# Two transformer blocks on one core: the up projections of MLP and FFN computed transposed, with the weights stationary

## The chip, the cores and the metric

One Trainium2 chip, one of its cores. The time is that of one execution on the device in microseconds; a lower one is better.

## The reference, cut to what matters

The program runs two transformer blocks in float32 on 256 tokens of width 2048. The first mixes by Fourier transform and attention and has an MLP with squared relu; the second (gated linear attention and a convolution, with modulation from a vector c) ends with a SwiGLU FFN. The parts that the change touches are these:

```python
    u = _rmsnorm(h, norm_mlp_g[layer])               # first block; D = 2048
    a = jnp.einsum('bsd,df->bsf', u, w_up[layer])    # 2048 -> 8192
    a = jnp.square(jax.nn.relu(a))
    h = h + jnp.einsum('bsf,fd->bsd', a, w_down[layer])
...
def swiglu(h, wg, wu, wd):                           # second block
    return (jax.nn.silu(h @ wg) * (h @ wu)) @ wd     # 2048 -> 5632 -> 2048
```

_rmsnorm scales every token by rsqrt(mean(x*x) + eps) and every channel by g.

## The kernel before, in words

**Precision.** A float32 matrix product is made of three fast ones. Each operand is split into a part rounded to float32r (whi, xhi, ahi, bhi) and a remainder (wlo, xlo, alo, blo); the products hi x hi, hi x lo and lo x hi are summed in PSUM.

**Weights.** SyncE streams all weights from HBM into a ring of four slots (wring), each a "group" of 4 depth tiles of 128 by 512 columns (512 KB), in two pieces of two tiles. For each piece ScalarE rounds to whi (round_groups, L488), VectorE subtracts to wlo (remainders, L919), TensorE multiplies. whi and wlo have room for 4 pieces, so the two engines work two groups ahead of TensorE. An engine's program is a fixed order written out by hand; counts kept by the class Counts turn it into semaphore waits.

**A block** is 512 output columns for all 256 tokens: four groups when the depth is 2048. multiply (L1514) holds 128 tokens of the activations stationary and streams 512 columns of weights: for each depth tile and each half t of the tokens three matmuls (L1530, L1531, L1532). So the sums lie in PSUM (acc, two banks for a pair) with tokens on the partitions and columns on the free axis. Two pairs of banks alternate.

**The MLP** (mlp_chunk, on PE L1693, ACT L692, DVE L1152) has 4 chunks of 2048 hidden columns. A chunk is four up blocks (j = 0 to 3, from ahi/alo) and four down blocks (j = 4 to 7, from xhi/xlo, 2048 deep). ScalarE's relu_square (L671) takes max(x, 0) * rstd out of PSUM, one operation for each half of the tokens (L676), and squares into blk (L680). For the down product the hidden columns must be on the partitions. So TensorE turns blk by 8 transposes of 128x128 (turn_rows, L1537, L1545) into the two banks of tp, beside the next block after its second group; ScalarE rounds from there into xhi (round_banks, L503) and VectorE takes the remainder (remain_banks, L959), which frees tp (tp_free). A down block is added to h by VectorE (add_block, L1122, L1124). Beside this VectorE multiplies the modulation matrix w_mod with two vectors, row by row, into macc (L935, L939); POOL loads it, and TensorE sums over partitions with ones (reduce_mod, L1555). The last chunk also turns the context rows for the second block.

**The FFN** (ffn, on PE L1935, ACT L862, DVE L1450) has 11 blocks of hidden columns in chunks of 4, 4 and 3. A hidden block is a gate block (pair 0) and an up block (pair 1). ScalarE takes silu of the gate out of PSUM into blk2 (silu_gate, L856), VectorE multiplies by the up sums out of PSUM into blk (gate_up, L1432, L1435), TensorE turns blk, and ScalarE and VectorE split it into bhi and blo. Four down blocks follow each chunk. The turn of a chunk's last block stands after the second group of the first down block, where its rounding and remainder are needed for the last group. The input of the FFN comes already normed and modulated in xhi/xlo; its first gate block is woven with the turning of the input (ffn_opening, L1916).

**Elsewhere**, which the change leaves alone: block l (multiply_rank, L1499, lines L1508 to L1510) is a projection to 32 columns that holds the 32 columns of weights stationary and streams 256 tokens, in float32r. The Fourier stage (L1608, L1619) has plain float32 matmuls with 128-column weights and about 128 streamed columns.

The loop over the hidden tiles in multiply, for comparison with the new one:

```python
for t in range(T):
    dst = acc[:, 2 * pair + t, :]
    rows = slice(t * P, (t + 1) * P)
    pe.matmul(dst, hi[:, tile, rows], whi[:, h4, w], start=(kg == first and k == 0), stop=False)
    pe.matmul(dst, hi[:, tile, rows], wlo[:, h4, w], start=False, stop=False)
```

## Time and profile before

| | us |
|---|---|
| median of 3 runs | 2341.2 (2340.49 to 2341.93) |
| the profiled execution | 2339.57 |
| its span | 2337.9 |
| TensorE busy | 2294.8 (98%) |
| TensorE's weight loads busy | 1891.3 (81%) |
| VectorE busy | 1541.3 (66%) |
| ScalarE busy | 1079.8 (46%) |

How to read it: PE is TensorE's matmuls, PEld its weight loads, which overlap the matmuls; DVE is VectorE, ACT ScalarE, POOL GpSimd. L1530 is line 1530 of the kernel. A row of a group has its count after x, then the busy time in us and the mean of one in ns, and then the engine's idle time before it. Matmuls are pipelined and the ends of their records are modelled, so the distance between starts, not the length of a record, tells how long one takes. The name on the left of <- is what is written.

### The profile page before, as it was taken

The numbers are of one execution on the slowest core, as the hardware profiler recorded it, in microseconds if no ns is written. First come the engines' busy times: TensorE is split into PE (matmuls) and PEld (weight loads), VectorE is DVE, ScalarE is ACT, GpSimd is POOL, SyncE is SP. The second block draws the span as 40 slices with busy tenths as digits, with TensorE's granted clock in tenths as the row PEclk, the third lists the DMA queues.
The fourth block names the chain that finished last, engine by engine and source line by source line (L and its number), as shares of the span: only waits on it lengthen the run. The fifth ranks groups of instructions, "written<-read, shape, count | busy, mean of one in ns | idle before, by whom it ended". The sixth has DMA issues, their size and how long they took to land.

```text
span 2337.9 us, 29147 instructions
## 1 busy us (share of the span) xinstructions
PE 2294.8 (98%) x10577; PEld 1891.3 (81%) x10577; DVE 1541.3 (66%) x1822; ACT 1079.8 (46%) x1291; POOL 146.2 (6%) x213
## 2 busy tenths in 40 slices
PE   8999999999999999999999999998999999999997
PEld 7887888888888888888878877787888888888886
DVE  7987658777876876886767664566455544455545
ACT  5445445445444444445563463444444344444444
POOL 1110001111111111110011000000000000000000
PEclk9999999999999999999999999999999999999999
DMA  9884458888888888886677663464555655555553
GB/s 340 291 273 155 127 180 300 294 306 272 271 295 267 264 289 272 268 279 215 214 250 242 210 210 126 145 242 154 195 184 191 209 194 188 190 195 188 193 180 108
DMA packets 245186, 523.91 MB, mean 224 GB/s; under 512 B 20016, under 2 KB 20288, under 8 KB 243776
## 3 DMA queue, kind: packets, MB, share of 16 engines
q1 hardware_dynamic: 213680, 404.80, 53.0%
q0 software_dynamic: 29568, 111.97, 13.9%
q10 hardware_dynamic: 1808, 5.37, 0.6%
q8 instruction: 86, 1.41, 0.3%
q14 instruction: 44, 0.36, 0.0%
HBM read 517.87 MB, written 4.21 MB: 223 GB/s over the span
## 4 chain that ended last, share of the span: by engine, by line
PE 97%; ACT 1%; DVE 1%; issue 1%; DMA 0%; ACTq 0%; DVEq 0%
PE acc L1530 30%; PE acc L1532 30%; PE acc L1531 30%; PE tp L1545 2%; PE m L1555 1%; PE acc L1665 0%; PE tp L1839 0%; PE tp L1857 0%; PE tp L1851 0%; PE acc L1629 0%; PE tp L1765 0%; PE m L1639 0%; PE tp L1825 0%; DVE wlo L919 0%; ACT whi L488 0%
## 5 line engine op out<-in xcount | busy, mean ns | idle before, releaser
L919 DVE TENSOR_TENSOR wlo<-wring,whi 128x1024 fp32r<-128x1024 f32 x776 | 935.1, 1214 | 603.9 <-ACT whi L488 600.6
L488 ACT ACTIVATE whi<-wring 128x1024 fp32r<-128x1024 f32 x776 | 813.5, 1052 | 1116.3 <-PE acc L1532 1113.0
L1530 PE MATMUL acc<-whi,xhi 128*128 128x512 f32 x2112 | 832.7, 394 | 2.7 <-issue 1.9
L1532 PE MATMUL acc<-whi,xlo 128*128 128x512 f32 x2112 | 823.4, 390 | 0.0
L1531 PE MATMUL acc<-wlo,xhi 128*128 128x512 f32 x2112 | 822.7, 390 | 0.0
L1530 PEld LDWEIGHTS acc<-whi,xhi 128*128 128x128 f32 x2112 | 397.2, 188 | 93.9 <-issue 12.7
L1532 PEld LDWEIGHTS acc<-whi,xlo 128*128 128x128 f32 x2112 | 396.8, 188 | 83.7
L1531 PEld LDWEIGHTS acc<-wlo,xhi 128*128 128x128 f32 x2112 | 397.4, 188 | 81.0 <-issue 0.7
L939 DVE SCALAR_TENSOR_TENSOR macc<-mring,csil,macc 128x512 f32<-128x512 f32 x480 | 344.2, 747 | 31.8 <-DMA mring<-w_mod 25.4
L1530 PE MATMUL acc<-whi,ahi 128*128 128x512 f32 x608 | 239.0, 393 | 2.0 <-DVE wlo L919 1.2
L1532 PE MATMUL acc<-whi,alo 128*128 128x512 f32 x608 | 237.0, 390 | 0.0
L1531 PE MATMUL acc<-wlo,ahi 128*128 128x512 f32 x608 | 236.6, 389 | 0.0
L427 POOL DMA_DIRECT2D mring<-w_mod x192 | 136.4, 711 | 1118.7 <-DVE macc L939 1097.2
L1530 PE MATMUL acc<-whi,bhi 128*128 128x512 f32 x352 | 137.2, 390 | 1.6 <-DVE blo L959 1.6
L1532 PE MATMUL acc<-whi,blo 128*128 128x512 f32 x352 | 137.0, 389 | 0.0
L1531 PE MATMUL acc<-wlo,bhi 128*128 128x512 f32 x352 | 136.9, 389 | 0.0
L1530 PEld LDWEIGHTS acc<-whi,ahi 128*128 128x128 f32 x608 | 114.2, 188 | 25.5 <-issue 2.7
L1532 PEld LDWEIGHTS acc<-whi,alo 128*128 128x128 f32 x608 | 114.1, 188 | 24.2
L1531 PEld LDWEIGHTS acc<-wlo,ahi 128*128 128x128 f32 x608 | 114.2, 188 | 23.0
L1530 PEld LDWEIGHTS acc<-whi,bhi 128*128 128x128 f32 x352 | 66.1, 188 | 15.4 <-DVE blo L959 1.8
L1532 PEld LDWEIGHTS acc<-whi,blo 128*128 128x128 f32 x352 | 66.1, 188 | 13.8
L1531 PEld LDWEIGHTS acc<-wlo,bhi 128*128 128x128 f32 x352 | 66.1, 188 | 13.6
(221 smaller groups left out, 1027.2 us busy)
## 6 DMA issues: line engine op xcount, KB each, us to landing
wring<-w_up SPq DMA_DIRECT2D x216, 512.0 KB, 4.6
wring<-w_down SPq DMA_DIRECT2D x216, 512.0 KB, 5.1
mring<-w_mod POOLq DMA_DIRECT2D x192, 512.0 KB, 5.2
wring<-w_in SPq DMA_DIRECT2D x184, 512.0 KB, 5.4
wring<-w_gate SPq DMA_DIRECT2D x88, 512.0 KB, 4.2
wring<-w_out SPq DMA_DIRECT2D x64, 512.0 KB, 4.8
gbig<-ctx_in POOLq DMA_DIRECT2D x2, 1024.0 KB, 8.3
hspill<-h ACTq DMA_DIRECT2D x1, 2048.0 KB, 7.9
```

The lines of the kernel that those rows point to most:

```text
L427: pool.dma_start(mring[:, c.slot("m", MSLOTS), :, :], w_mod_v[s, :, :, bass.ds(i * NB + kind * D, NB)])\
L488: act.activation(whi[:, piece_slot(c, piece), 0:half], wring[:, g4, piece * half:(piece + 1) * half], ACT.Copy).then_inc(hi_done, 1)
L919: dve.tensor_tensor(wlo[:, h4, 0:half], wring[:, g4, piece * half:(piece + 1) * half], whi[:, h4, 0:half].bitcast(F32), ALU.subtract).then ...
L939: dve.scalar_tensor_tensor(macc[:, who, :], mring[:, m2, kt, :], csil[:, who, k:k + 1], macc[:, who, :], ALU.mult, ALU.add).then_inc(mod_a ...
L1530: pe.matmul(dst, hi[:, tile, rows], whi[:, h4, w], start=(kg == first and k == 0), stop=False)
L1531: pe.matmul(dst, hi[:, tile, rows], wlo[:, h4, w], start=False, stop=False)
L1532: last = pe.matmul(dst, lo[:, tile, rows], whi[:, h4, w], start=False, stop=(kg == final and k == KG - 1))
L1545: last = pe.transpose(tp[:, q, j * S + t * P:j * S + (t + 1) * P], src[:, t, f:f + P], ident)
L1555: last = pe.matmul(m1[:, 4 * who + j:4 * who + j + 1], macc[:, who, j * P:(j + 1) * P], ones[:, 0:1], start=True, stop=True)
```

## The change

The up projections (MLP) and the gate and up projections (FFN) are computed with the weights stationary. multiply_turned holds 128 columns of weights and streams all 256 tokens, so that the sums come out with hidden columns on the partitions and tokens on the free axis: for a depth tile 4 slices of columns times three matmuls of 256 instead of 2 halves of the tokens times three of 512. Two slices share a bank. blk then has the form that the down product needs; it is not turned. ScalarE rounds it by one operation from blk (round_up), VectorE takes the remainder by one (remainder_up), and the semaphores up_hi and up_lo stand for them. Since tokens lie on the free axis, relu can't take rstd as a scale of the partitions any more; relu_square leaves it out, and the adds of the down blocks multiply by rsq = rstd * rstd (add_scaled). The down blocks stay as they were. The core of the diff:

```diff
@@ -668,17 +672,20 @@
             round_added(3)
             square_added(3 * NB, 3)
 
-            def relu_square(j, first=False):
-
-                if first:
-                    act.wait_ge(rstd_done, 2)
-                for t in range(T):
-                    last = act.activation(blk2[:, t, :], acc[:, 2 * (j % 2) + t, :], ACT.Relu, scale=rstd[:, 1, t:t + 1])
-                last.then_inc(blk_half, 1)
+            def relu_square(j):
+
+                act.wait_ge(up_lo, c.at("up"))
+                act.activation(blk2[:, :, :], acc[:, 2 * (j % 2):2 * (j % 2) + 2, :], ACT.Relu).then_inc(blk_half, 1)
                 c.add("half")
                 act.wait_ge(blk_half, c.at("half"))
                 act.activation(blk[:, :, :], blk2[:, :, :], ACT.Square).then_inc(blk_ready, 1)
                 c.add("blk")
+
+            def round_up(dst, tile):
+
+                act.wait_ge(blk_ready, c.at("blk"))
+                act.activation(dst[:, tile:tile + 4, :], blk_tiles, ACT.Copy).then_inc(up_hi, 1)
+                c.add("up")
 
             def square_block(n, first):
 
...
@@ -1125,6 +1132,20 @@
                                   ALU.add).then_inc(h_added, 1)
 
 
+            def add_scaled(n, pair):
+
+                for t in range(T):
+                    cols = h[:, t, n:n + NB]
+                    last = dve.scalar_tensor_tensor(cols, acc[:, 2 * pair + t, :], rsq[:, t:t + 1], cols, ALU.mult, ALU.add)
+                last.then_inc(h_added, 1)
+
+            def remainder_up(hi, lo, tile):
+
+                c.add("up")
+                dve.wait_ge(up_hi, c.at("up"))
+                dve.tensor_tensor(lo[:, tile:tile + 4, :], blk_tiles, hi[:, tile:tile + 4, :].bitcast(F32),
+                                  ALU.subtract).then_inc(up_lo, 1)
+
             def remain_added(n):
 
                 remain_banks(ahi, alo, 4 * n, 2, lambda k: vecs[:, 0, V_MLPG + k:V_MLPG + k + 1])
...
@@ -1159,8 +1180,10 @@
                         norm_mean(1)
                     elif first and g == 2:
                         norm_root(1, mean=False)
+                        dve.tensor_tensor(rsq[:, :], rstd[:, 1, :], rstd[:, 1, :], ALU.mult).then_inc(rsq_set, 1)
+                        dve.wait_ge(rsq_set, 1)
                     if g % 4 == 1 and 1 <= j <= 4:
-                        remain_banks(xhi, xlo, 4 * (j - 1), 2)
+                        remainder_up(xhi, xlo, 4 * (j - 1))
                     if g in MLP_REDUCED:
                         set_mod(MLP_REDUCED[g], i, MLP_REDUCED[g] == SC1)
                         if last and MLP_REDUCED[g] == SC1:
...
@@ -1432,6 +1455,7 @@
             def gate_up():
 
                 dve.wait_ge(blk_half, c.at("half", 1))
+                dve.wait_ge(up_lo, c.at("up"))
                 dve.tensor_tensor(blk[:, :, :], blk2[:, :, :], acc[:, 2:4, :], ALU.mult).then_inc(blk_ready, 1)
                 c.add("half")
 
...
@@ -1531,6 +1555,26 @@
                                 pe.matmul(dst, hi[:, tile, rows], wlo[:, h4, w], start=False, stop=False)
                                 last = pe.matmul(dst, lo[:, tile, rows], whi[:, h4, w], start=False,
                                                  stop=(kg == final and k == KG - 1))
+                        last.then_inc(piece_multiplied, 1)
+                    c.add("g")
+
+            def multiply_turned(hi, lo, kgs, pair, operand=None):
+
+                for kg in kgs:
+                    for piece in range(SPLIT):
+                        h4 = piece_slot(c, piece)
+                        if operand:
+                            pe.wait_ge(operand[0], operand[1] + piece)
+                        pe.wait_ge(lo_done, c.at("g", SPLIT * WSLOTS + piece + 1, SPLIT))
+                        for j in range(HALF):
+                            tile = kg * KG + piece * HALF + j
+                            for f in range(NB // P):
+                                dst = acc[:, 2 * pair + f // 2, f % 2 * S:(f % 2 + 1) * S]
+                                w = slice(j * NB + f * P, j * NB + (f + 1) * P)
+                                pe.matmul(dst, whi[:, h4, w], hi[:, tile, :], start=(tile == 0 and f % 2 == 0), stop=False)
+                                pe.matmul(dst, whi[:, h4, w], lo[:, tile, :], start=False, stop=False)
+                                last = pe.matmul(dst, wlo[:, h4, w], hi[:, tile, :], start=False,
+                                                 stop=(tile == KT - 1 and f % 2 == 1))
                         last.then_inc(piece_multiplied, 1)
                     c.add("g")
 
...
@@ -1707,20 +1751,26 @@
                         pe.wait_ge(blk_half, c.at("half", j - 1))
                     else:
                         pe.wait_ge(h_added, c.at("ha", 2 + j - 5))
-                    hi, lo = (ahi, alo) if j < 4 else (xhi, xlo)
+                    def group(kg):
+
+                        if j < 4:
+                            multiply_turned(ahi, alo, (kg,), pair)
+                        else:
+                            if j == 4:
+                                c.add("up")
+                                pe.wait_ge(up_lo, c.at("up"))
+                            multiply(xhi, xlo, (kg,), 4, pair)
+
                     for kg in range(3):
-                        multiply(hi, lo, (kg,), 4, pair)
+                        group(kg)
                         if first and j == 0 and kg == 0:
                             turn_added(3)
-                        if kg == 1 and 1 <= j <= 4:
-                            pe.wait_ge(blk_ready, c.at("blk", j))
-                            turn_rows(blk, 2)
                         if 4 * j + kg in MLP_REDUCED:
                             reduce_kind(MLP_REDUCED[4 * j + kg])
                         turn_ctx(4 * j + kg)
-                    if j == 4 or (first and j == 0):
+                    if first and j == 0:
                         pe.wait_ge(tp_free, c.at("q", 2))
-                    multiply(hi, lo, (3,), 4, pair)
+                    group(3)
                     if 4 * j + 3 in MLP_REDUCED:
                         reduce_kind(MLP_REDUCED[4 * j + 3])
                     turn_ctx(4 * j + 3)
...
@@ -1941,26 +1991,19 @@
                     if first and j == 0:
                         ffn_opening()
                     else:
-                        multiply(xhi, xlo, range(2), 4, 0)
-                        if j:
-                            pe.wait_ge(blk_ready, c.at("blk", j))
-                            turn_rows(blk, 2)
-                        multiply(xhi, xlo, (2, 3), 4, 0)
+                        multiply_turned(xhi, xlo, range(4), 0)
                     if not j:
                         pe.wait_ge(h_scaled, c.at("hs"))
-                    multiply(xhi, xlo, range(4), 4, 1)
+                    multiply_turned(xhi, xlo, range(4), 1)
                 for n in range(4):
                     if n == 0:
                         pe.wait_ge(blk_half, c.at("half", blocks))
                     elif n >= 2:
                         pe.wait_ge(h_scaled, c.at("hs", n - 1))
-                    multiply(bhi, blo, range(2), blocks, n % 2)
-                    if n == 0:
-                        pe.wait_ge(blk_ready, c.at("blk", blocks))
-                        turn_rows(blk, 2)
-                    for kg in range(2, blocks):
-                        if n == 0 and kg == blocks - 1:
-                            pe.wait_ge(tp_free, c.at("q", 2))
+                    for kg in range(blocks):
+                        if n == 0:
+                            c.add("up")
+                            pe.wait_ge(up_lo, c.at("up"))
                         multiply(bhi, blo, (kg,), blocks, n % 2)
                 c.add("half", blocks)
                 c.add("blk", blocks)
```

Not shown: the tile rsq and the semaphores are declared; round_banks and remain_banks of blk become round_up and remainder_up at the same places of ScalarE's and VectorE's orders (in mlp_chunk and ffn); add_block of the MLP's down blocks becomes add_scaled; the four calls of multiply in TensorE's ffn_opening become multiply_turned; counts of the loops follow.

## Rows read from the trace of the kernel before

**Rows 1.** the page's busy times (part 1) and granted clock (part 2)
```profile
PE 2294.8 (98%) x10577; PEld 1891.3 (81%) x10577; DVE 1541.3 (66%) x1822; ACT 1079.8 (46%) x1291; POOL 146.2 (6%) x213
...
PEclk9999999999999999999999999999999999999999
```
**Rows 2.** the page's chain that ended last, by line
```profile
PE acc L1530 30%; PE acc L1532 30%; PE acc L1531 30%; PE tp L1545 2%; PE m L1555 1%; PE acc L1665 0%; PE tp L1839 0%; PE tp L1857 0%; PE tp L1851 0%; PE acc L1629 0%; PE tp L1765 0%; PE m L1639 0%; PE tp L1825 0%; DVE wlo L919 0%; ACT whi L488 0%
```
**Rows 3.** list of TensorE's waits: us in total, times, longest
```profile
PE acc L1530 <- DVE blo L959: 1.6, 1, 1.6
```
**Rows 4.** busy times in two stretches: us, then each engine's busy us
```profile
core 0: us, PE busy (x) PEld busy (x) DVE busy (x) ACT busy (x) POOL busy (x), PEclk, DMA share, GB/s
340.00:523.00 183.00, 183.00 (x848) 152.47 (x847) 141.81 (x168) 88.38 (x106) 24.38 (x35) 1.00 0.86 294
1606.00:1860.00 254.00, 254.00 (x1139) 210.67 (x1138) 133.00 (x117) 108.35 (x108) 0.00 (x0) 1.00 0.58 192
```
**Rows 5.** timeline of TensorE in an up block: start us, us, instruction
```profile
899.62 0.39 PE L1530 MATMUL acc<-whi,ahi 128*128 128x512 f32 x1
...
905.97 0.39 PE L1531 MATMUL acc<-wlo,ahi 128*128 128x512 f32 x1
```
**Rows 6.** TensorE groups by line and form: busy us, mean ns, idle before
```profile
L1530 PEld LDWEIGHTS acc<-whi,xhi 128*128 128x128 f32 x2112 | 397.2, 188 | 93.9 <-issue 12.7 <-DVE xlo L979 0.7 <-DVE wlo L919 0.4
...
L1508 PEld LDWEIGHTS acc<-xhi,whi 128*32 128x32 f32 x16 | 1.7, 108 | 0.1
...
L1545 PE MATMUL tp<-tabs,blk 128*128 128x128 f32 x248 | 32.2, 273 | 0.1
```
**Rows 7.** timeline of TensorE around one turn of blk
```profile
373.68 1.04 PE L1545 MATMUL tp<-tabs,blk 128*128 128x128 f32 x8
...
374.47 0.47 PE L1530 MATMUL acc<-whi,ahi 128*128 128x512 f32 x1
...
377.09 0.39 PE L1532 MATMUL acc<-whi,alo 128*128 128x512 f32 x1
```
**Rows 8.** timeline, last FFN chunk: VectorE, then TensorE
```profile
2259.66 1.22 DVE L1435 TENSOR_TENSOR blk<-blk,acc 128x1024 f32<-128x1024 f32 x1
...
2268.05 1.03 PE L1545 MATMUL tp<-tabs,blk 128*128 128x128 f32 x8
...
2270.66 0.50 PE L1530 MATMUL acc<-whi,bhi 128*128 128x512 f32 x1 [1.57 <-DVE blo L959]
```
**Rows 9.** timeline of TensorE in block l: first, fourth and last of 48
```profile
1097.33 0.28 PE L1508 MATMUL acc<-ahi,whi 128*32 128x256 f32 x1
...
1097.68 0.28 PE L1508 MATMUL acc<-ahi,whi 128*32 128x256 f32 x1
...
1102.67 0.28 PE L1510 MATMUL acc<-alo,whi 128*32 128x256 f32 x1
```
**Rows 10.** timeline in the Fourier stage: matmuls, then their weight loads
```profile
197.12 1.95 PE L1608 MATMUL acc<-tab_f,proj 128*128 128x129 f32 x16
...
197.01 1.86 PEld L1608 LDWEIGHTS acc<-tab_f,proj 128*128 128x128 f32 x16
```
**Rows 11.** VectorE groups by line and form: busy us, mean ns, idle before
```profile
L939 DVE SCALAR_TENSOR_TENSOR macc<-mring,csil,macc 128x512 f32<-128x512 f32 x480 | 344.2, 747 | 31.8 <-DMA mring<-w_mod 25.4 <-DVE states L1277 0.7 <-DVE convT L1218 0.4
...
L959 DVE TENSOR_TENSOR xlo<-tp,xhi 128x512 fp32r<-128x512 f32 x32 | 20.5, 682 | 0.0
...
L1239 DVE SCALAR_TENSOR_TENSOR gbig<-tp,gbig 128x512 f32<-128x512 f32 x8 | 5.5, 692 | 19.5 <-ACT gbig L768 19.5
...
L1331 DVE TENSOR_TENSOR xlo<-convT,xhi 128x1024 fp32r<-128x1024 f32 x2 | 2.4, 1222 | 2.1 <-ACT xhi L819 2.1
```
**Rows 12.** timeline of TensorE, one reduction of macc by ones
```profile
933.87 0.95 PE L1555 MATMUL m<-ones,macc 128*128 128x1 f32 x8
```
**Rows 13.** the page's DMA queues (part 3) and issues (part 6)
```profile
q8 instruction: 86, 1.41, 0.3%
...
wring<-w_in SPq DMA_DIRECT2D x8, 64.0 KB, 2.4
```

40 lines of the change are left out of this document (22 added, 18 removed).

## Prediction, made before the change was run

> **What bounds the kernel now.** I read the page's head first: TensorE is busy for 98% of the span, and the granted clock is at its upper level in all 40 slices [rows 1]. The chain of work that ended last says the same: nine tenths of it are the three matmul lines of the big products [rows 2]. TensorE waits for little. In the list of its waits only one lies in the stretches that change, 1.6 us for blo [rows 3]. VectorE and ScalarE have room: 141.8 and 88.4 of 183 us in the first MLP chunk, 133.0 and 108.4 of 254 in the first FFN chunk [rows 4]. So the kernel lasts as long as TensorE's stream, and every edit is priced by what it does to the spacing of matmul starts. The length of a matmul's record (0.39 us) is not that price, since the records overlap.
>
> **The spacing now.** Between two starts that are 28 matmuls apart lie 905.97 - 899.62 = 6.35 us, 226.8 ns each, for 512 columns [rows 5]. A weight load's record is 188 ns long [rows 6]; it lies beside the matmul before and costs nothing, with 39 ns to spare.
>
> **Part 1, the transposes go.** A block of 512 hidden columns is turned by 8 transposes. There are 16 such blocks in the MLP and 11 in the FFN, so 27 x 8 = 216 of the 248 in the row of tp<-tabs,blk [rows 6]. On TensorE's path: the transposes start at 373.68, and the twelfth matmul behind them at 377.09 [rows 7]. Without them that one would start 11 x 226.8 ns behind 373.68, at 376.17. One turn thus costs 0.92 us: 0.79 up to the next start, the rest in slower intervals behind it. I round to 0.90: 27 x 0.90 = 24.3 us, all of it on the path, since TensorE is the chain. In the last FFN chunk the turn is followed by the wait for blo: transposes at 2268.05, next matmul at 2270.66, 2.61 us instead of 0.79 [rows 8], another 1.8 us. Sum: 26.1 us off.
>
> **Part 2, the turned matmuls.** There are 16 up blocks in the MLP and 22 gate and up blocks in the FFN, 38 in all. Each has 16 tiles of the depth with 2 x 3 matmuls of 512 columns, and gets 4 x 3 of 256: 3648 matmuls of 512 become 7296 of 256, each with a weight load of 128 columns. The columns streamed are the same; the question is the spacing at 256. The nearest row is the small product of 32 columns (block l), which has this form already, with narrow weights: from 1097.33 to 1102.67 are 47 spacings in 5.34 us, 113.6 ns each [rows 9], as good as half of 226.8. So a matmul has next to no fixed cost of its own. What this row does not show is the wide load: its loads last 108 ns, ours 188 [rows 6]. For that, the Fourier stage: 16 matmuls, each with a load of 128 columns, take (1.95 - 0.275)/15 = 111.7 ns each (0.275 is the last one's own record), and their loads (1.86 - 0.19)/15 = 111.3 each, though a load's record there lasts 0.19 as well [rows 10]. So loads overlap one another's tail, and a wide load needs 111.3 ns of spacing at least; that is 2 ns under 113.6. Lower end for the spacing: 113.3, half of 226.7; the columns have to be streamed, so it can't be less. Upper end: if a load had to end before its matmul starts and begin with the matmul before, at least 188 ns. The Fourier rows have the very same width of weights and contradict that, so I take 113.6. For the range I keep 117, the spacing at the beginning of the narrow run, (1097.68 - 1097.33)/3 [rows 9]. Cost: 7296 x 113.6 = 828.8 us against 3648 x 226.8 = 827.4, +1.4 us. Each further nanosecond costs 7.3 us, and at 117 the gain is gone (853.6 - 827.4 = +26.2).
>
> The Trainium skill ("TensorE: Matmul & The Clock Gate", section "LDWEIGHTS (loading the stationary operand)") puts a load at its columns divided by 1.2 GHz, an estimate of 106.7 ns for 128; the trace's 111.3 is longer. With the page's figure 7 ns of the spacing would stay free instead of 2, and the sum would be the same.
>
> **Part 3, ScalarE and VectorE.** Per hidden block ScalarE rounds and, in the MLP, rectifies the same elements in half the instructions, so it does no more than now. On VectorE two remainders of 682 become one of 1222, and in the MLP an add of the same size (1.22) becomes two scaled adds, priced by the scalar_tensor_tensor on 512 elements of PSUM at 692 each [rows 11]: (1.222 + 1.384) - (1.364 + 1.222) = +0.02 us a block. In the last chunk of the MLP the add ahead of the next norm ends 0.16 later; the blocks behind it on TensorE read the context, which is long ready. The product rsq is one operation on two elements and one wait on VectorE in the first chunk; queued behind it are the remainders of the weights, which are two groups ahead of TensorE. I cost all of this at nothing. The cover is VectorE's free fifth in the MLP [rows 4]; without it the 16 blocks would cost 16 x 0.02 = 0.3 us. SP's and POOL's queues issue the same transfers in the same order, and what releases them (pieces multiplied, macc steps) keeps its pace.
>
> **Part 4, the new waits.** Relu waits for up_lo, the remainder of the block before, because blk must be free; that remainder is made beside the third group of the block, and relu comes behind its fourth. The FFN's gate_up on VectorE waits for its own engine's count, done 30 us before; the weight remainders behind it are not held. TensorE waits for up_lo ahead of each group of the first down block. The last of these is critical, 7 times in all (4 MLP chunks, 3 FFN). The rounding on ScalarE comes behind the weight rounding that needs the group two before; from that point TensorE has one group, 24 x 226.8 = 5.44 us, and the steps are about 1.05 (weights) + 1.05 + 1.22 = 3.3 us. In the MLP VectorE may first have two w_mod steps of 747 ns to finish [rows 11]; that still fits. In the last FFN chunk, which has three groups, the block is ready when gate_up ends, 2259.66 + 1.22 = 2260.88 [rows 8]; one weight rounding and one weight remainder come between, and by the same durations blo is there some 2 us before 2268.05. Today the rounding can only begin behind the transposes, hence that wait. Cost 0; if all seven waited as today's one does, 7 x 1.6 = 11 us.
>
> **Sum:** -26.1 + 1.4 = -24.7 us. The profiled execution took 2339.6 us for a span of 2337.9, so it would take 2314.9. The median of the three runs, 2341.2, is 1.6 above it, and I carry that over: 2316.5.
>
> **Rivals.**
> (a) The weight load becomes the bound. For it: only 2 ns of room, all 7296 pairs hang on it, and no row has a wide load beside a full-rate stream of 256 columns: the Fourier rows have plain float32, whose 128 columns take as long as 256 of ours. Against it: with a wide load every 227 ns and with a narrow one every 114 the stream has the same 0.443 ns per column [rows 5, 9]. Price: by eight reductions of a single column, where the load is all there is, 0.95 us, 119 ns each with their ends [rows 12]: 7296 x 119 = 868.2, +40.8 us, 2341.2 - 26.1 + 40.8 = 2355.9. It decides from a spacing of 117, and its tail goes to 188 ns (1371.6 - 827.4 = +544 us). Chance 0.10.
> The Trainium skill (same page, section "Back-to-back issue gap") has a rule that speaks for this rival: loads and matmuls together set the spacing, about 81 ns at 128 columns where a matmul alone takes 56. An estimate from it, 25 ns on top of 113.6 for 7296 pairs, is +184 us. The Fourier rows show no such surcharge: 111.7 is no more than the load alone [rows 10].
> (b) Instructions do not come fast enough. TensorE gets 3648 - 216 = 3432 more matmuls, each with a load. The longest run at this density now has 48 pairs [rows 9]; the FFN will have 1536 in a row. The instruction queue brought 86 packets [rows 13]; if some 50 for these stretches were each exposed by 2.4 us, the landing of a small transfer, that is +120 us, about 2436; ten of them would take the gain. Against: those 48 pairs keep one even spacing to their end. Chance 0.03.
> (c) The turn's wait stays in another guise: seven hand-overs at 1.6 us, 2316.5 + 11 = 2328. For: that is what the last one does now; against: the 2 us of room above. Chance 0.06.
> (d) The spacing is 116 to 117, and it cancels: some 2336.5 to 2342. Chance 0.05.
>
> **How the numbers follow.** The forecast has 0.76 and (c) 0.06, so faster by over 0.2% is 0.82. (d), 0.05, is within 0.2% (4.7 us, about what a measurement of this kernel can tell from no change). (a) and (b), 0.13, are slower. The range goes from 2312 (turns at 0.92, spacing 113.3, and 2 us for the scatter of runs) to 2340 (spacing near 116.5, or both (c) and 115); left out are (a), (b) and a part of (d), under 2 in 10.
>
> **What would show it.** Of tp<-tabs,blk 32 transposes are left. The turned matmuls start 113 to 114 ns apart for hundreds in a row, and the loads' share is near 100% there. An up block of the MLP, 96 x 226.8 ns + 0.9 us = 22.7 us now, takes 21.8; a gate and up pair of the FFN 43.6 instead of 44.4. The wait for blo is gone. Wrong would be: a spacing of 117 or more in the up blocks (a), gaps put down to issue every few us (b), a wait for xlo or blo by the last group of the first down block (c).

## The result, and the profile after

The changed kernel takes **2362.2 us** (median of 4 runs, 2360.1 to 2364.3), the kernel before 2341.2 on the same chip: ratio **1.0089**, 95% interval 1.0073 to 1.0105. The change is slower by 21 us. The forecast was 2316.5 and its range ended at 2340, so the prediction was wrong by 46 us and in its sign. The profiled execution has a span of 2358.4 us against 2337.9, 20.5 more, and the sums below are made against that. Every time given is the median of undisturbed executions; one of the four of a_aligned, below, took 3297.1 us at a mean granted clock of 0.65 and is left aside.

The page of the changed kernel, busy times, granted clock, chain and instruction queue, answers to [rows 1, 2, 13]:

```profile
PE 2316.8 (98%) x14009; PEld 2049.7 (87%) x14009; DVE 1542.1 (65%) x1812; ACT 1075.4 (46%) x1248; POOL 146.6 (6%) x213
...
PEclk9999999999999999999999999999999999999999
...
q8 instruction: 112, 1.84, 0.3%
...
PE acc L1554 18%; PE acc L1556 17%; PE acc L1555 17%; PE acc L1574 12%; PE acc L1576 12%; PE acc L1575 12%; PE m L1599 1%; PE tp L1589 1%; DVE wlo L926 0%; PE acc L1709 0%; PE tp L1889 0%; DMA h<-x 0%; PE tp L1907 0%; PE tp L1901 0%; PE acc L1673 0%
```

TensorE is still the chain, and its granted clock reads 9 (90% of full speed or more) in every slice, as before. The new line numbers are 1554 to 1556 (multiply, stationary tokens) and 1574 to 1576 (multiply_turned, stationary weights). The instruction queue brought 26 packets more than before.

Its waits (us in total, times, longest) answer to [rows 3]:

```profile
PE acc L1554 <- DVE wlo L926: 1.5, 2, 1.0
PE tp L1589 <- DVE xlo L970: 1.4, 1, 1.4
PE m L1865 <- ACT gate_cols L782: 1.3, 1, 1.3
PE m L1599 <- DVE macc L946: 1.3, 1, 1.3
```

The wait for blo is gone, and none for up_lo has come in its place. The row "PE m <- DVE macc" is new and worth 1.3 us, once; the other three are in the kernel before as well. So the time did not come in as waits. It came in as spacing. Busy time in windows that lie wholly inside one kind of matmul (us, then TensorE's busy us and its count of instructions, the granted clock, the DMA share and GB/s):

```profile
386.00:426.00 40.00, 40.00 (x346) 1.00 0.87 294
472.00:512.00 40.00, 40.00 (x178) 1.00 0.89 311
1610.00:1770.00 160.00, 160.00 (x1336) 1.00 0.58 185
1785.00:1855.00 70.00, 70.00 (x301) 1.00 0.58 185
```

and of the kernel before, an FFN down block and an FFN up block:

```profile
1785.00:1855.00 70.00, 70.00 (x310) 1.00 0.57 188
1651.00:1691.00 40.00, 40.00 (x178) 1.00 0.56 186
```

A count takes in the one to three records that overlap the window's ends. The windows of after are, in order, a turned block of the MLP, a down block of the MLP, the first turned stretch of the FFN and a down block of the FFN. Read them by length over count: turned matmuls near 116 and near 120 ns, where 113.6 was forecast; the MLP's down block as the FFN up block of before, which holds the same tile xhi (178 in 40 us both times); the FFN's down block, which the change doesn't touch, has only 301 where 310 stood before. The exact spacings come from the timeline of the changed kernel:

```profile
1604.03 0.36 PE L1574 MATMUL acc<-xhi,whi 128*128 128x256 f32 x1
...
1776.90 0.40 PE L1554 MATMUL acc<-whi,bhi 128*128 128x512 f32 x1
...
1866.49 0.28 PE L1574 MATMUL acc<-xhi,whi 128*128 128x256 f32 x1
```

Between the first two lie the 1440 matmuls of 4 gate and up pairs less the opening's first groups: 172.87 us, **120.0 ns** each, without a gap. Between the second and the third lie 384 of the down blocks: 89.59 us, **233.3 ns** each, where [rows 5] had 226.8. The mean distance between starts over all neighbours of a kind, before and after: turned xhi 120.0, turned ahi 117.0 (half of the 227.1 of before is 113.5); stationary bhi 226.8 and then 233.3; stationary ahi (the 288 matmuls of the blocks behind the MLP) 227.1 and 233.1; stationary xhi 227.1 and 227.2.

Where the 20.5 us came from:

- turned xhi: 4224 x (120.0 - 113.5) = +27.5
- turned ahi: 3072 x (117.0 - 113.5) = +10.8
- stationary bhi: 1056 x (233.3 - 226.8) = +6.9
- stationary ahi: 288 x (233.1 - 227.1) = +1.7
- 27 turns and the last wait gone: -24.3 - 1.8 = -26.1

Sum +20.8. Two things had to be explained: why a turned matmul takes 3.5 to 6.5 ns more than half a wide one, and why down blocks that nobody edited became slower.

For the second the kernels differ in one respect. The new tile rsq is 8 bytes wide, sits ahead of blk and takes a slot of 32 bytes, so blk and every tile behind it (blk2, tmpT, ahi, alo, bhi, blo) lies 32 bytes further on in SBUF; whi, wlo, xhi and xlo stay. Below, **shift** is the distance of a token tile from whi, modulo 256 bytes, against the one it has in the kernel before; there, by the declared sizes of the tiles between them, xhi lies 61440 bytes (240 x 256) and ahi and bhi 114432 bytes (447 x 256) behind whi, whole multiples of 256.

### The profile page after: what moved, and what is told of

Its sections match the earlier page's. It is cut to its first block, busy times and chain, and to the rows that moved or that the text cites. A ratio compares the mean times of both kernels' runs of the same rounds, so it can differ in the third digit from the quotient of the medians.

```text
span 2358.4 us, 35923 instructions
## 1 busy us (share of the span) xinstructions
PE 2316.8 (98%) x14009; PEld 2049.7 (87%) x14009; DVE 1542.1 (65%) x1812; ACT 1075.4 (46%) x1248; POOL 146.6 (6%) x213
## 4 chain that ended last, share of the span: by engine, by line
PE 96%; DVE 1%; ACT 1%; issue 1%; DMA 1%; ACTq 0%; DVEq 0%; POOLq 0%
PE acc L1554 18%; PE acc L1556 17%; PE acc L1555 17%; PE acc L1574 12%; PE acc L1576 12%; PE acc L1575 12%; PE m L1599 1%; PE tp L1589 1%; DVE wlo L926 0%; PE acc L1709 0%; PE tp L1889 0%; DMA h<-x 0%; PE tp L1907 0%; PE tp L1901 0%; PE acc L1673 0%
## 5 line engine op out<-in xcount | busy, mean ns | idle before, releaser
L1554 PE MATMUL acc<-whi,xhi 128*128 128x512 f32 x1408 | 556.8, 395 | 2.5 <-issue 1.9
L1556 PE MATMUL acc<-whi,xlo 128*128 128x512 f32 x1408 | 549.0, 390 | 0.0
L1555 PE MATMUL acc<-wlo,xhi 128*128 128x512 f32 x1408 | 548.3, 389 | 0.0
L1574 PE MATMUL acc<-xhi,whi 128*128 128x256 f32 x1408 | 398.9, 283 | 0.1
L1575 PE MATMUL acc<-xlo,whi 128*128 128x256 f32 x1408 | 398.5, 283 | 0.0
L1576 PE MATMUL acc<-xhi,wlo 128*128 128x256 f32 x1408 | 398.4, 283 | 0.0
L1554 PEld LDWEIGHTS acc<-whi,xhi 128*128 128x128 f32 x1408 | 264.6, 188 | 65.9 <-issue 12.7
L1574 PE MATMUL acc<-ahi,whi 128*128 128x256 f32 x1024 | 286.3, 280 | 0.0
L1576 PE MATMUL acc<-ahi,wlo 128*128 128x256 f32 x1024 | 285.9, 279 | 0.0
L1575 PE MATMUL acc<-alo,whi 128*128 128x256 f32 x1024 | 285.6, 279 | 0.0
L1574 PEld LDWEIGHTS acc<-xhi,whi 128*128 128x128 f32 x1408 | 270.4, 192 | 0.6 <-DVE xlo L986 0.5
```

The lines of the kernel that those rows point to most:

```text
L1556: last = pe.matmul(dst, lo[:, tile, rows], whi[:, h4, w], start=False, stop=(kg == final and k == KG - 1))
L1574: pe.matmul(dst, whi[:, h4, w], hi[:, tile, :], start=(tile == 0 and f % 2 == 0), stop=False)
L1575: pe.matmul(dst, whi[:, h4, w], lo[:, tile, :], start=False, stop=False)
L1576: last = pe.matmul(dst, wlo[:, h4, w], hi[:, tile, :], start=False, stop=(tile == KT - 1 and f % 2 == 1))
```

## The experiments

Theory F (fixed piece): a load of 128 columns adds a fixed time to the stream, whatever its length. Theory P (placement): the shift of the stationary against the streamed tile sets that time. Rival C: the cost is proportional to the columns. Rival L: the loads alone are the bound, as in (a) of the prediction.

**a_aligned.** The change with the addresses of before: rsq becomes a row of rstd.

```diff
-        rstd = sb("rstd", [P, 7, T])
-        rsq = sb("rsq", [P, T])
+        rstd = sb("rstd", [P, 8, T])
+        rsq = rstd[:, 7, :]
```

> The changed kernel, with rsq placed inside a tile that exists already, so that blk and all tiles behind it (ahi, alo, bhi, blo) have their addresses of before, multiples of 64 bytes; in the changed kernel the new tile shifted them by 32. Placement theory (a shift by 32 bytes changes what a pair of load and matmul costs): the FFN's down blocks go back from 233.3 to 227 ns a matmul (-6.7 us), the matmuls with ahi stationary behind the MLP too (-1.9), and the MLP's up blocks go from 116.9 to the 120 of the FFN's (3072 x 3.1 = +9.5): about the same total, 2363. Rival (the turned stretch leaves TensorE's stream in a slower state for what follows): nothing moves, 233.3 in the down blocks and 116.9 in the MLP stay.

Measured 2362.9 against 2340.2, ratio 1.0095 (1.0075 to 1.0115). Windows of a turned MLP block, a turned FFN stretch and an FFN down block:

```profile
388.00:428.00 40.00, 40.00 (x335) 1.00 0.85 280
...
1620.00:1780.00 160.00, 160.00 (x1336) 1.00 0.58 186
1795.00:1865.00 70.00, 70.00 (x310) 1.00 0.60 195
```

The down block has its 310 back (226.7 ns). The turned MLP block falls from 346 to 335, which is 120.0 ns, as in the FFN. So rsq's 32 bytes cost the down blocks 6.5 ns a matmul and gave the MLP's turned ones 3. With everything in its old place the sum closes: 7296 x 120.0 - 827.4 = +48.1, less 26.1, is +22.0; measured +22.7. (Spacings of 427 ns at a granted clock of 0.50, near 1029 us, add some 1.3 us in this run's trace; the changed kernel has none there.)

**b_off.** The kernel before, with 32 bytes ahead of blk and nothing else.

```diff
+        sb("pad", [P, 8])
         blk = sb("blk", [P, T, NB])
```

> The kernel before, with 32 bytes left free ahead of blk, so that ahi, alo, bhi and blo lie where the changed kernel has them. Placement theory: all 2880 matmuls with them stationary go from 226.8 to about 233.3 ns, +18.7 us, 2360. Rival (it is the turned stretch that slows what follows): 2341, no change.

Measured 2359.2, ratio 1.008 (1.0063 to 1.0097). An MLP down block (stationary xhi, not shifted) and an FFN down block (stationary bhi, shifted):

```profile
476.00:516.00 40.00, 40.00 (x178) 1.00 0.89 303
1800.00:1870.00 70.00, 70.00 (x302) 1.00 0.57 189
```

Placement alone makes the kernel before 19 us slower. No other edit is in this run, so P is shown for stationary tiles, as a fact; why the shift matters is not.

**b_w_off.** The kernel before; two small tiles move ahead, so that whi and wlo lie 32 bytes further on, xhi and xlo 64, ahi and bhi stay.

```diff
+        ones = sb("ones", [P, 1])
         whi = sb("whi", [P, HSLOTS, HALF * NB], F32R)
         wlo = sb("wlo", [P, HSLOTS, HALF * NB], F32R)
+        squares = sb("squares", [P, T, KG])
...
-        ones = sb("ones", [P, 1])
...
-        squares = sb("squares", [P, T, KG])
```

> The kernel before, with whi and wlo shifted by 32 bytes and all other big tiles as they were; there they are the streamed operand. If a shifted streamed operand costs less beside an aligned stationary one, as 116.9 against 120 in the changed kernel suggests, a matmul of 512 columns goes from 226.8 to about 223.5, 9216 x 3.3 = -30 us, 2311. If only equal placement of both is good (the mixed case of the down blocks), 233.3, +60 us, 2401. If the streamed operand's place does not matter, 2341.

Measured 2395.1, ratio 1.0236 (1.0219 to 1.0253). The same two kinds of block:

```profile
482.00:522.00 40.00, 40.00 (x173) 1.00 0.87 299
1825.00:1895.00 70.00, 70.00 (x302) 1.00 0.57 182
```

Now xhi (shift 32) is slow too: 173 instead of 178, 233.3 ns. ahi and bhi are at a shift of -32, that is 224, and as slow.

**b_wx_off.** Is it the address or the distance? whi, wlo, xhi and xlo all 32 bytes further on (only ones moves), ahi and bhi in place.

> The kernel before with whi, wlo and xhi, xlo all shifted by 32 bytes, ahi to blo in place. If what matters is that the streamed and the stationary operand have the same place within 64 bytes: 226.8 ns with xhi stationary (both shifted) and 233.3 with ahi and bhi (one shifted), +19 us, 2359. If every shifted operand costs by itself: 233 or more with xhi too, +60 us or more, 2400.

Measured 2356.9 (one run).

```profile
475.00:515.00 40.00, 40.00 (x178) 1.00 0.92 303
1800.00:1870.00 70.00, 70.00 (x302) 1.00 0.57 186
```

xhi, which moved together with whi, is fast; bhi, which did not move, is slow. The distance counts.

**m_sizes.** The aligned change, with 384 columns streamed in the MLP and 192 in the FFN for each load of 128.

```diff
+                            cols = 384 if hi is ahi else 192
+                            two = min(tile, KT - 2)
+                            mhi = hi[:, two:two + 2, :].rearrange("p a s -> p (a s)")[:, 0:cols]
...
-                                dst = acc[:, 2 * pair + f // 2, f % 2 * S:(f % 2 + 1) * S]
+                                dst = acc[:, 2 * pair + f // 2, 0:cols]
```

> As a_aligned, but the turned matmuls stream 384 columns in the MLP and 192 in the FFN instead of 256, of two neighbouring depth tiles, so the products are not the reference's; loads, weights and order stay. Theory that each wide load takes a fixed piece of about 13.3 ns out of the stream: 384/2.4 + 13.3 = 173.3 ns in the MLP, and in the FFN 80 + 13.3 = 93.3, which is under what loads need, so about 111.5. Rival, the load can't come oftener than every 120 ns beside a stream: 120 in the FFN, and in the MLP 160 to 170. What the prediction assumed, 0.443 ns a column: 170.0 in the MLP and 111.5 in the FFN.

This kernel took 2493.1 us (one run; it streams more in the MLP). Windows in the MLP and in the FFN:

```profile
410.00:470.00 60.00, 60.00 (x348) 1.00 0.62 202
1785.00:1925.00 140.00, 140.00 (x1256) 1.00 0.63 203
```

384 columns take 173.3 ns, 192 take 111.8. The stream alone would need 160.0 and 80.0 (columns over the 2.4 GHz of the upper level). With 512 at 226.7 (213.3) and 256 at 120.0 (106.7), three lengths have the same surcharge of 13.3 ns. That is F, not C. All three stand at shift 0. The 192 columns would need 80.0 + 13.3 = 93.3 and take 111.8, near the 111.3 of [rows 10]; I read this as the spacing that the loads need by themselves. At 256 columns, with 120.0, they are then not the bound: L falls. The Trainium skill ("TensorE: Matmul & The Clock Gate", section "LDWEIGHTS (loading the stationary operand)") gives an estimate of 106.7 ns for such a load; the trace's 111.8 is 5 ns longer.

**m_widths.** The same, with 256 columns streamed and a load of 96 columns in the MLP, of 64 in the FFN.

```diff
-                                dst = acc[:, 2 * pair + f // 2, f % 2 * S:(f % 2 + 1) * S]
-                                w = slice(j * NB + f * P, j * NB + (f + 1) * P)
+                                wide = 96 if hi is ahi else 64
+                                dst = acc[0:wide, 2 * pair + f // 2, f % 2 * S:(f % 2 + 1) * S]
+                                w = slice(j * NB + f * P, j * NB + f * P + wide)
```

> As a_aligned, but the turned matmuls hold only the first 96 of each 128 columns of weights in the MLP and the first 64 in the FFN, so a part of the hidden columns is left out; 256 tokens are streamed as before. The piece that a load takes out of the stream is 13.3 ns with 128 columns and 6.7 with 32 (block l). If it grows with the columns of the load: 8.9 with 64 and 11.1 with 96, that is 115.6 ns in the FFN and 117.8 in the MLP. If it is fixed for every load that is not narrow: 120 in both. What the prediction assumed (no piece at all, 0.443 ns a streamed column): 113.4 in both.

```profile
388.00:428.00 40.00, 40.00 (x347) 1.00 0.89 300
1610.00:1760.00 150.00, 150.00 (x1326) 1.00 0.61 197
```

The kernel took 2326.1 us (one run). A load of 64 columns gives 113.4 ns, one of 96 gives 116.2. With the 32 columns of [rows 9] the surcharge is 6.7 ns up to 64 columns, 9.5 at 96, 13.3 at 128. Neither of the expected forms came, a surcharge proportional to the width or one fixed for every load that is not narrow. This is the point that the prediction missed: its narrow row stood on the lower step, its wide row on the upper one. Two limits: a wider load also writes more partitions of PSUM, and no run separates the two; and all these widths were compared at shift 0. At shift 32 the width makes no such difference. In the changed kernel, where ahi lies at 32, block l (load of 32 columns, 256 streamed) starts its first and its last of 48 matmuls here:

```profile
1093.60 0.28 PE L1532 MATMUL acc<-ahi,whi 128*32 128x256 f32 x1
...
1099.12 0.28 PE L1534 MATMUL acc<-alo,whi 128*32 128x256 f32 x1
```

These are 47 spacings in 5.52 us, 117.3 ns each before rounding, where [rows 9] had 113.6 and the wide loads on ahi take 117.0.

**m_few_turns.** What are the turns worth by themselves? The kernel before, each turn of blk with 2 transposes in place of 8 (the rest of blk stays unturned).

```diff
-                    for j in range(2):
-                        for t in range(T):
+                    for j in range(1 if few else 2):
+                        for t in range(1 if few else T):
```

> The kernel before with 2 instead of 8 transposes in each of the 27 turns of blk, so most of the operand of the down products is not turned and the output is not the reference's. If a turn's price is on the path: 27 x 6 x 0.109 = -17.7 us. If part of it covers a wait that follows (the rounding of the turned block), less, down to nothing.

Measured 2327.4 against 2340.1: 12.7 us less, ratio 0.9946 (0.9927 to 0.9964), where 17.7 was expected. Windows behind a reduction of macc (the granted clock stands behind the count):

```profile
611.70:614.70 3.00, 3.00 (x8) 0.50 0.86 289
614.70:618.00 3.30, 3.30 (x15) 0.95 0.90 315
973.50:976.60 3.10, 3.10 (x9) 0.50 0.85 297
```

and the timeline of the first of them:

```profile
609.09 1.95 PE L1555 MATMUL m<-ones,macc 128*128 128x1 f32 x16
610.90 0.48 PE L1530 MATMUL acc<-whi,xhi 128*128 128x512 f32 x1
...
611.72 0.63 PE L1530 MATMUL acc<-whi,xhi 128*128 128x512 f32 x1
612.14 0.63 PE L1531 MATMUL acc<-wlo,xhi 128*128 128x512 f32 x1
```

Behind 16 matmuls of one column in 1.8 us the granted clock is at its lower level, 1.2 GHz, for 3 us, and seven matmuls start 427 ns apart instead of 227: 1.4 us lost. It happens three times in this run: at 612 and 974 behind such a reduction, at 1486 behind an idle stretch of 1.9 us. The kernel before and the changed kernel have the same two reductions (before at 614 and 980 us) and the same idle stretch, and in neither does the clock fall behind them; what decides it is not shown. The three are 4.2 us of the 5.0 that are missing; a wait of 1.0 us for macc, which the kernel before does not have, is about the rest. The turns are worth what the prediction said; the clock took part of it back here.

**mlp_only, mlp_only_2.** The MLP turned, the FFN as before. In the first ahi lies at shift 32 and bhi at 64, in the second bhi at 128.

```diff
+        rsq = sb("rsq", [P, T])
         blk = sb("blk", [P, T, NB])
...
+            sb("padb", [P, 8], scope=ph)
             bhi = sb("bhi", [P, KT, S], F32R, scope=ph)
```

> The changed kernel with the FFN as it was before: turned matmuls and no transposes in the MLP alone. ahi and alo stay shifted by 32 bytes as in the changed kernel, where their turned matmuls took 116.9 ns instead of 120; bhi and blo are put back on a multiple of 64. If the cost of a wide load and the price of a turn are what the traces show: -16 x 0.9 = -14.4 us for the turns, 3072 x 116.9 - 1536 x 226.8 = +10.8 for the matmuls, 288 x 6.5 ns = +1.9 for the blocks behind the MLP that hold ahi stationary: -1.7 us, no change that can be measured. If placement only shifts cost about and the turned form always costs 120: +7.8.

> mlp_only once more, with bhi and blo on a multiple of 128 bytes instead of 64; ahi and alo stay shifted by 32. The first mlp_only took 6.3 us more than the kernel before where -1.7 was expected, and its down blocks of the FFN, on a multiple of 64, ran at 233.3 ns instead of 226.7, 1056 x 6.6 = 7.0 us. With that gone: -0.7 to -1.7 us against the kernel before, 2339, no change that can be measured. If it stays at +6, the cause lies elsewhere, in the MLP.

Both expectations failed: 2346.4 (1.0025, 1.0015 to 1.0035) and 2344.2 (1.0014, 1.0005 to 1.0023). A shift of 64 leaves bhi at 233.3 ns and one of 128 at 232.4, so neither is as good as 0. The second kernel's down block:

```profile
1785.00:1855.00 70.00, 70.00 (x303) 1.00 0.56 185
```

**p_x32_a64, p_x64_a96, p_x128_a192.** The full change at other shifts, named in the labels (xhi and xlo; ahi and bhi). The moves are of small tiles, as in b_w_off; for example

```diff
+        ones = sb("ones", [P, 1])
+        squares = sb("squares", [P, T, KG])
         xhi = sb("xhi", [P, KT, S], F32R)
...
+        sb("pad", [P, 24])
         blk = sb("blk", [P, T, NB])
```

> The same with xhi, xlo shifted by 32 and ahi to blo by 64. Reads that meet in parts of 128 bytes: 116.9 for the FFN's turned matmuls (so far 120 there, shift 0) and 233.3 for those that hold xhi, 116.9 and 233.3 with ahi. If 64 is a special place: another value with ahi.

> The changed kernel with xhi, xlo shifted by 64 bytes against whi, wlo, and ahi to blo by 96 (addresses modulo 128). Known so far: shift 0 gives 120.0 ns for the turned matmuls and 226.7 for those of 512 columns, shift 32 gives 116.9 and 233.3, shift 64 gives 233.3 for 512 (the FFN's down blocks of mlp_only). If the streamed and the stationary reads meet in parts of 128 bytes, 32, 64 and 96 are alike: 116.9 and 233.3 for both tiles, in all 2341 + 22 + 4 + 28 = some 2385. If 64 or 96 is a better place for the turned form, its spacing there is near 113.4, and a version that puts its streamed operand there could beat both kernels. If only 32 is special, 64 and 96 give 120.

> The full change, with xhi, xlo shifted by 128 bytes against whi, and ahi, bhi by 192 (modulo 256; 0 is their place in the kernel before). Shifts of 32, 64 and 96 gave turned spacings of 117, 115 to 118 and 120, and 233 for stationary tiles at each of them. Theory 1, the placement costs a stationary tile the same 6.5 ns at every shift but 0, and a turned stream a little more or less around 117: x turned 115 to 120, a turned 115 to 120, stationary 233 for both; then no placement brings the turned form to 113.4, and the change can't win by placement alone; time 2370 to 2378. Theory 2, shift 128 is a second good place in which the load and the stream never meet: x turned about 113.4, then 4224 x 6.6 ns = 28 us less in the FFN's turned blocks than at 120, and x stationary either 226.7 or 233: 2335 to 2350.

Measured 2374.2 (1.0141, 1.0123 to 1.016), 2376.7 (1.0152, 1.0133 to 1.0171) and 2372.7 (one run). They are slower because the 4224 matmuls that hold xhi or xlo now take 232.5 to 233.3 ns. The view that matters is p_x64_a96's, the first turned stretch of the FFN and the second:

```profile
1650.00:1800.00 150.00, 150.00 (x1276) 1.00 0.58 189
1905.00:2065.00 160.00, 160.00 (x1414) 1.00 0.61 202
```

The same instructions on the same tiles take 117.8 ns each in the one and **113.3** in the other, from their beginning to their end. The first is entered from transposes, the second (and the third) from the down blocks. In p_x128_a192 two turned blocks of the MLP differ in the same way:

```profile
393.00:433.00 40.00, 40.00 (x355) 1.00 0.87 300
576.00:616.00 40.00, 40.00 (x342) 1.00 0.86 287
```

So the 13.3 ns are not the price of a wide load as such: they are its price at shift 0, and 113.3, the forecast's spacing, can be reached. All shifts together, as mean spacings in ns ("or" where whole stretches differ; the last column is block l):

```
shift   stationary tokens, 512 columns   turned, 256 columns   load of 32, 256 columns
0       226.7 to 227.4 (a, b, x)         120.0 (a, x)          113.6
32      233.1 to 233.4                   116.7 or 117.8        117.3
64      233.3 to 233.4                   117.8 or 113.3        114.0
96      234.1 to 234.3                   120.0                 116.8
128     232.4, 232.5                     118.7 or 120.0        113.6
192     228.9 to 230.5                   117.8 or 113.3        113.6, 113.8
224     233.3 to 233.6                   not tried             116.7
```

The two forms want opposite things: stationary tokens are fastest at 0, turned matmuls with a load of 128 slowest there (and at 96). The narrow load follows neither: it is near 114 at 0, 64, 128 and 192 and near 117 at 32, 96 and 224.

**mlp_only_3, mlp_only_4.** The MLP turned, with bhi back at shift 0 and ahi at 32, then at 192.

```diff
+            sb("pada", [P, 8], scope=ph)
             ahi = sb("ahi", [P, KT, S], F32R, scope=ph)
...
+            sb("padg", [P, 8], scope=ph)
             gbig = sb("gbig", [P, 2 * D], scope=ph)
```

> The change in the MLP alone, with the two placements that the other runs found better for each form: ahi and alo 32 bytes further on than before (the turned matmuls of the MLP took 117 ns there instead of 120), bhi and blo exactly where they are in the kernel before, 447 x 256 bytes behind whi (the 1056 matmuls of the FFN's down blocks that hold bhi took 226.7 ns there, and 233 when shifted by 32, 64 or 128 bytes). Theory of placement, with a period of 256 bytes: the down blocks are back at 226.7 +- 0.3, the turned ones stay at 117.0, and against mlp_only_2 the 1056 matmuls give back 5.6 to 6.5 ns each, 5.9 to 6.9 us: 2337.3 to 2338.3, ratio 0.998 to 0.999, so this version would be the first to beat the kernel before, by about 3 us. If the gain of the 16 turns of the MLP (14.4 us by the prediction's price) is given back to a late VectorE as in the run with few transposes, mlp_only_2 would already contain that, and the number is the same. Rival: it is the scope's first tile or the presence of the other edits that slows the down blocks, not the address: they stay at 233, time 2344.

> As mlp_only_3, but with ahi, alo 64 bytes nearer to whi than in the kernel before (a shift of 192 modulo 256) instead of 32 further away, and xhi, bhi at their distance to whi as before. In the run with that shift the turned matmuls of the MLP took 115.7 ns, against 116.9 in mlp_only_3, and stationary ahi 230.5 against 233.1. If distance to whi is all that counts: 3072 x 1.2 + 288 x 2.6 ns = 4.4 us less than mlp_only_3, 2335, ratio about 0.998, with x and b stationary at 226.8 to 227.1, though all of whi, wlo, xhi and xlo now lie 64 bytes further on. Rival: the spacing of 115.7 belonged to another thing in that run (its xhi at 128, or the absolute address); then the turned matmuls take 117 or 120 and the time is 2339 to 2348.

mlp_only_3: 2339.5 against 2340.4, ratio 0.9993 (0.9984 to 1.0002). A turned block and an FFN down block:

```profile
388.00:428.00 40.00, 40.00 (x346) 1.00 0.87 294
1785.00:1855.00 70.00, 70.00 (x311) 1.00 0.58 190
```

bhi is at 226.8 again and ahi at 116.9, as expected, and the +3.3 us of mlp_only_2 against its own runs of before have become -0.9. It is no faster than before beyond the measurement: 3072 x (116.9 - 113.5) = +10.4, stationary ahi +1.7, 16 turns -14.4, sum -2.3, measured -0.9. One place gives some back:

```profile
1018.13 1.05 PE L1600 MATMUL m<-ones,macc 128*128 128x1 f32 x8 [1.31 <-DVE macc L948]
...
1020.22 0.63 PE L1557 MATMUL acc<-whi,xlo 128*128 128x512 f32 x1
1020.65 0.63 PE L1555 MATMUL acc<-whi,xhi 128*128 128x512 f32 x1
```

a wait of 1.3 us for macc, and behind it again 427 ns a matmul at half the clock (the changed kernel has the same wait and the same eight matmuls at 1017 us, and no lower clock behind them). mlp_only_4 took 2339.6, ratio 0.9992 (0.9983 to 1.0001): its turned matmuls all take 117.8, not the mean of 115.7 that the same shift had in p_x128_a192. The expected 2335 failed, and with it the idea that the distance to whi alone picks the value; the expectation's rival, 2339 to 2348, came.

**f_x64, f_x192.** The full change with each operand at its best shift: two views of one tile, so that the FFN's tokens lie 64 bytes from xhi's place (further on, or nearer), and everything that is held stationary, but for ahi's 288 matmuls, is at 0.

```diff
-        xhi = sb("xhi", [P, KT, S], F32R)
-        xlo = sb("xlo", [P, KT, S], F32R)
+        xs = sb("xs", [P, 2 * KT * S + 16], F32R)
+        xhi, xlo = [xs[:, n * KT * S + 0:(n + 1) * KT * S + 0].rearrange("p (k s) -> p k s", k=KT) for n in range(2)]
+        fhi, flo = [xs[:, n * KT * S + 16:(n + 1) * KT * S + 16].rearrange("p (k s) -> p k s", k=KT) for n in range(2)]
```

> The full change, with each operand at the distance to the weights that suits its form: in the FFN the normalized tokens are written 64 bytes further on (two views of one tile), so that the turned matmuls stream them at a shift of 64, while xhi in the MLP's down blocks and bhi in the FFN's, which are held stationary, keep their distance of before; ahi is shifted by 32 as in the changed kernel. In the run with xhi at 64 and ahi at 96 the first stretch of the FFN (1440 matmuls, entered from transposes) took 117.8 ns each and the two later ones (1536 and 1152, entered from the down blocks) 113.3. Theory 1, the shift sets the few spacings that are possible and the way a stretch is entered picks one: the same here. Against the kernel before, the FFN pays 1440 x 117.8 + 2784 x 113.3 - 2112 x 226.9 ns = +5.9 us and is spared 11 turns and the last wait, 9.9 + 1.8 = 11.7 us: -5.8; the MLP as in mlp_only_3, -0.9. Time 2334.5 (2331 to 2338), ratio 0.997, the first version faster than both kernels; stationary x and b at 227.1 and 226.8. Theory 2, the 113.3 came with that run's slower down blocks (234 ns), so with bhi back in place the later stretches take 117.8 as well: 2784 x 4.5 = 12.5 us more, 2347.

> As f_x64, but in the FFN the tokens lie 64 bytes nearer to the weights instead (192 modulo 256). In the MLP that shift of ahi gave 117.8 in five blocks and 113.3 in three in one run and 117.8 in all in another. If shifts of 64 and 192 are mirror images: spacings of 117.8 or 113.3 in the FFN's stretches, time 2334 to 2347. If not: 116.7 as at 32, or 120 as at 0 and 128; time up to 2356.

Measured 2345.8 (1.0023, 1.0014 to 1.0032) and 2345.9 (1.0016, 1.0006 to 1.0026). f_x64's windows, a turned block of the MLP and the first and second stretch of the FFN:

```profile
386.00:426.00 40.00, 40.00 (x345) 1.00 0.88 301
1610.00:1770.00 160.00, 160.00 (x1361) 1.00 0.59 191
1870.00:2030.00 160.00, 160.00 (x1360) 1.00 0.57 187
```

All stretches of the FFN take 117.8 ns, also those entered from the down blocks, and theory 2 of this run's expectation holds. Placement alone, with the whole change in, is worth 16.4 us (2362.2 to 2345.8). It doesn't make the change a gain, since the change pays only under a spacing of 117.0. In neither run did a stretch come at 113.3. One of the 8 executions of f_x192 took 2338.3 where the others took 2343 to 2350; a long stretch at 113.3 (1536 x 4.5 ns = 6.9 us) would do that, but that execution has no profile, so its cause is not shown.

## Why the prediction was wrong

**Part 2 failed; it is 37 of the 45 us between forecast and trace.** The step was: "So a matmul has next to no fixed cost of its own", and in (a) "with a wide load every 227 ns and with a narrow one every 114 the stream has the same 0.443 ns per column". The two rows differ in two things at once, the columns streamed and the width of the load, and the two differences happen to cancel. 226.8 is 213.3 + 13.3 with a load of 128 columns, 113.6 is 106.7 + 6.7 with one of 32 (m_sizes, m_widths). Half the columns with the wide load is 106.7 + 13.3 = 120.0 at the old placement, which the FFN's turned matmuls kept. The MLP's lie at shift 32, where wide and narrow loads both take about 117; there the row of block l was off by its placement and not by its width. The term was sized at +1.4 us and measured +38.3 (27.5 + 10.8), and +48.1 in a_aligned, where no placement helps it. The prediction noted that no row showed a wide load at that length and that each nanosecond costs 7.3 us, and still gave the case a tenth. The fact in hand that should have spoken: 226.8 against the 213.3 that 512 columns take at 2.4 GHz leaves 13.5 ns unexplained in every matmul, and a cost per matmul doubles when the matmuls do.

**What is not touched stays as it is** was assumed without a word; it is the other 8.6 us. rsq moved every tile behind it by 32 bytes: +6.9 on the FFN's down blocks, +1.7 behind the MLP, and, against a_aligned, 3072 x 3.0 = -9.2 in the turned MLP blocks. The three nearly cancel, so a_aligned and the changed kernel take the same time by different sums.

**Part 1 was right.** 27 turns and the last wait are gone, and the closing sums want them at their 26.1 us: +22.0 against the +22.7 of a_aligned, +20.8 against the +20.5 here. m_few_turns kept 12.7 of its 17.7, the rest going to the clock (4.2), which the changed kernel did not suffer, and to the wait for macc (1.0).

**Part 3 was right in effect.** The groups of VectorE in the changed kernel:

```profile
L1139 DVE SCALAR_TENSOR_TENSOR h<-acc,rsq,h 128x512 f32<-128x512 f32 x32 | 22.5, 744 | 14.0 <-PE acc L1556 14.0
L1146 DVE TENSOR_TENSOR xlo<-blk,xhi 128x1024 fp32r<-128x1024 f32 x16 | 19.5, 1217 | 0.0
```

A scaled add takes 744 ns, not the 692 of [rows 11], and VectorE's sum is 1542.1 us against 1541.3. The single wait for macc, 1.3 us, need not be its mark: m_few_turns has no scaled add and waits there too, for 1.0 us.

**Part 4 was right**: no wait for up_lo. Rival (c) did not come.

**Rival (a)** had the side and nearly the size: 119 ns and 2355.9 us, against 117.0 to 120.0 and 2362.2. Its mechanism was not the one at work: the loads alone need 111.8. The page's rule beside it (the Trainium skill, "TensorE: Matmul & The Clock Gate", section "Back-to-back issue gap") gives an estimate of 25 ns; the sign is borne out, and the 3.5 to 6.5 ns measured are about a quarter of that at most.

**Rival (b)** did not come: 26 more packets of instructions, and 1440 matmuls in one even spacing. **(d)** describes what the MLP alone became in mlp_only_3, a draw.

What stays open: why the shift matters, and what picks 113.3 or 117.8 for a whole stretch at one and the same shift. Entry from a slow down block went with 113.3 in p_x64_a96 and entry from a fast one with 117.8 in f_x64, but p_x128_a192's MLP has both. No version that computes the whole result is faster than the kernel before beyond the interval; mlp_only_3 and mlp_only_4 equal it.

## What to carry to other kernels

Before splitting matmuls, take the spacing apart: columns over the granted clock, and the rest, which each additional matmul pays again; two rows whose cost per column agrees prove nothing if they differ in the width of the load too. A new tile of 8 bytes can move every tile behind it: when matmuls that nobody edited change their spacing, compare the addresses first, and put small additions behind the large operands or inside an existing tile. When TensorE is the bound, the distance between the stationary and the streamed tile is worth a scan of its own.

## What the runs showed of the hardware that was not expected

- The surcharge on the stream at the upper clock (float32r): 13.3 ns for a load of 128 columns at shift 0, whether 256, 384 or 512 columns are streamed; 6.7 ns for 32 or 64 columns. At shift 32, with 256 streamed, a load of 32 and one of 128 both take about 117 ns in all.
- The distance between stationary and streamed tile, modulo at least 256 bytes: 226.7 or 228.9 to 234.3 ns for 512 columns, 120.0 down to 113.3 for 256. In the kernel before it is worth 19 us (b_off) to 55 us (b_w_off).
- Turned matmuls keep one spacing for a whole stretch of 384 to 1536, and the next stretch of the same instructions can have another (117.8, then 113.3).
- Sixteen matmuls of one column in 1.8 us were followed by 3 us at a granted clock of 0.50 twice in m_few_turns; at the same places of the kernel before and of the changed one the clock stayed at its upper level.
